# Summed squares as a rounded high and low part, summed behind the fourth weight block; a bank of their own for five first outputs

## The reference

```
def rms_norm(x, w):
    xf = x.astype(jnp.float32)
    y = xf * lax.rsqrt(jnp.mean(xf * xf, axis=-1, keepdims=True) + EPS)
    return (y * w.astype(jnp.float32)).astype(x.dtype)

for layer in range(DEPTH):
    h = rms_norm(x, norm_mix_pre[layer])
    m = mixer_block(h, ...)
    x = x + rms_norm(m, norm_mix_post[layer])
    h = rms_norm(x, norm_ffn_pre[layer])
    f = (silu(h @ w_gate) * (h @ w_up)) @ w_down
    x = x + rms_norm(f, norm_ffn_post[layer])
```

## Time and profile before

| What | us |
|---|---|
| Median of 3 runs (2761.96 to 2762.15) | 2762.11 |
| The profiled execution | 2762.7 |
| Its span, first to last instruction | 2760.9 |
| PE busy | 2743.2 |
| DVE busy | 1517.9 |
| ACT busy | 1051.0 |

### The profile page before, as it was taken

One profiled execution on the slowest core, in us unless ns is written; L12 is line 12 of the kernel. 1 busy time (PEld: TensorE's weight loads), 2 busy tenths in 40 slices (PEclk: granted clock), 3 DMA queues, 4 the chain that ended last, 5 costly groups with the idle time before them and its releaser, 6 DMA issues.

```text
span 2760.9 us, 36069 instructions
## 1 busy us (share of the span) xinstructions
PE 2743.2 (99%) x13580; PEld 2285.3 (83%) x13580; DVE 1517.9 (55%) x2147; ACT 1051.0 (38%) x1462; POOL 57.0 (2%) x59
## 2 busy tenths in 40 slices
PE   9999999999999999999999999999999999999998
PEld 7887888888888888788888888988888877888887
DVE  6944655654434784555565443554434798654433
ACT  5335443432223533633343232332222467432221
POOL 0030000000000003000000000000000000000000
PEclk9999999999999999999999999999999999999999
DMA  4242333233332224133323333233333330233332
GB/s 146 84 125 62 95 92 107 77 108 97 97 98 88 84 88 119 55 102 95 111 76 107 96 91 103 74 113 93 97 97 92 115 106 5 73 114 94 94 99 79
DMA packets 80152, 258.68 MB, mean 94 GB/s; under 512 B 9936, under 2 KB 12368, under 8 KB 79536
## 3 DMA queue, kind: packets, MB, share of 16 engines
q1 hardware_dynamic: 74160, 248.57, 30.2%
q10 hardware_dynamic: 5888, 8.68, 1.2%
HBM read 247.51 MB, written 2.10 MB: 90 GB/s over the span
## 4 chain that ended last, share of the span: by engine, by line
PE 98%; DVE 1%; ACT 1%; issue 0%; DMA 0%; ACTq 0%; DVEq 0%; SPq 0%
PE bank L440 30%; PE bank L441 30%; PE bank L442 30%; PE bank L1344 1%; PE bank L1322 1%; PE bank L1105 1%; PE bank L1308 1%; PE bank L1121 1%; PE bank L1152 1%; DVE w_lo L610 0%; PE bank L1133 0%; PE bank L506 0%; PE bank L514 0%; DVE x L768 0%; ACT w_hi L606 0%
## 5 line engine op out<-in xcount | busy, mean ns | idle before, releaser
L440 PE MATMUL bank<-u_hi,w_hi 128*128 128x512 f32 (+1 forms) x2640 | 1004.3, 380 | 5.4 <-DVE scratch L874 2.7
L441 PE MATMUL bank<-u_lo,w_hi 128*128 128x512 f32 (+1 forms) x2640 | 993.7, 376 | 0.0
L442 PE MATMUL bank<-u_hi,w_lo 128*128 128x512 f32 (+1 forms) x2640 | 993.5, 376 | 0.0
L610 DVE TENSOR_TENSOR w_lo<-raw,w_hi 128x1024 fp32r<-128x1024 f32 x490 | 604.0, 1233 | 616.2 <-ACT w_hi L606 604.8
L606 ACT ACTIVATE w_hi<-raw 128x1024 fp32r<-128x1024 f32 x490 | 514.7, 1050 | 345.8 <-PE bank L442 315.4
L440 PEld LDWEIGHTS bank<-u_hi,w_hi 128*128 128x128 f32 x2640 | 496.9, 188 | 104.8 <-DVE w_lo L610 5.8
L441 PEld LDWEIGHTS bank<-u_lo,w_hi 128*128 128x128 f32 x2640 | 496.9, 188 | 91.3 <-issue 2.4
L442 PEld LDWEIGHTS bank<-u_hi,w_lo 128*128 128x128 f32 x2640 | 496.8, 188 | 91.3
L440 PE MATMUL bank<-hid_hi,w_hi 128*128 128x512 f32 (+1 forms) x792 | 290.1, 366 | 0.0
L442 PE MATMUL bank<-hid_hi,w_lo 128*128 128x512 f32 (+1 forms) x792 | 289.4, 365 | 0.0
L441 PE MATMUL bank<-hid_lo,w_hi 128*128 128x512 f32 (+1 forms) x792 | 289.4, 365 | 0.0
(11 more groups left out here) (273 smaller groups left out, 2594.4 us busy)
## 6 DMA issues: line engine op xcount, KB each, us to landing
raw<-in_weights SPq DMA_DIRECT2D x410, 512.0 KB, 3.5
raw<-in_weights SPq DMA_DIRECT2D x48, 256.0 KB, 2.7
raw<-in_weights SPq DMA_DIRECT2D x32, 384.0 KB, 3.1
rot_s<-rot_in ACTq DMA_DIRECT2D x32, 128.0 KB, 2.3
q_s<-q_in ACTq DMA_DIRECT2D x52, 64.0 KB, 3.0
x<-in_x SPq DMA_DIRECT2D x4, 512.0 KB, 6.6
ret_mask<-in_ret_mask SPq DMA_DIRECT2D x2, 1024.0 KB, 6.0
out<-x SPq DMA_DIRECT2D x16, 128.0 KB, 1.8
```

Source lines behind the costliest of these rows:

```text
L440: nc.tensor.matmul(out, st_hi, mv_hi, start=first, stop=False)
L441: nc.tensor.matmul(out, st_hi, mv_lo, start=False, stop=False)
L442: return nc.tensor.matmul(out, st_lo, mv_hi, start=False, stop=last)
L610: nc.vector.tensor_tensor(w_lo[:, bl.slot(p), :], raw[:, bl.raw(p), :], w_hi[:, bl.slot(p), :].bitcast(F32), ALU.subtract).then_inc(lo_spl ...
```

## The change

Four things are changed.

1. The "pre" sum is no longer a float32 matmul of `acc`. ACT rounds `acc` into `sq_hi[:, 0, :]` (`act_acc_high`), DVE subtracts the rounded part and writes the rest into `sq_hi[:, 1, :]` (`dve_acc_low`), and PE makes two float32r matmuls with `ones_r`. Both new instructions stand behind the split of block 4, and PE waits for the low part before the first of the two.
2. The sum stands behind the whole of block 3, not before its k = 6.
3. The same split is made at each join for the share of `acc` in the half sums; the squares that came last stay in float32.
4. In stages 1, 3, 4, 5 and 6 the stage's first output goes into bank 4 instead of its place in the round; the first matmul itself raises the counter of the bank that is passed over.

`ones_r` is written at the start of layer 0 instead of in each layer's first head copy.

```
+FIRST_BANK = 4
+FIRST_NO = {1: 0, 3: 1, 4: 2, 5: 3, 6: 4}
...
         def pe_sums_pre(pe, key, s, li=None):
             use = side(key, li)
             pe.wait_ge(use.drained, use.n + 1)
-            pe.wait_ge(acc_done.sem, acc_done.upto(s, 7))
-            nc.tensor.matmul(use.mem[:, :], ones_c, acc[:, :], start=True, stop=True).then_inc(use.filled, 1)
+            pe.wait_ge(acc_lo.sem, acc_lo.upto(s, 1))
+            nc.tensor.matmul(use.mem[:, :], ones_r[:, :], sq_hi[:, 0, :], start=True, stop=False)
+            nc.tensor.matmul(use.mem[:, :], ones_r[:, :], sq_hi[:, 1, :], start=False, stop=True).then_inc(use.filled, 1)
...
         def pe_sums_half(pe, key, s, hf, paired, li=None):
-            pe.wait_ge(acc_done.sem, acc_done.upto(s, 13))
-            nc.tensor.matmul(use.mem[:, 0:TH], ones_c, acc[:, cols], start=True, stop=False)
+            pe.wait_ge(acc_lo.sem, acc_lo.upto(s, 2))
+            nc.tensor.matmul(use.mem[:, 0:TH], ones_r[:, :], sq_hi[:, 0, cols], start=True, stop=False)
+            nc.tensor.matmul(use.mem[:, 0:TH], ones_r[:, :], sq_hi[:, 1, cols], start=False, stop=False)
...
+        def first_result(s):
+            return Use(ps[FIRST_BANK], first_out.sem, None, first_out.upto(FIRST_NO[s], -1))
...
         def pe_first(pe, bl, ou, s, sums_b):
+            beside = s in FIRST_NO
...
+                to = ps[FIRST_BANK] if beside and i == 0 else ps[ou.bank(i)]
...
+                    if beside and i == 0 and hf == 0 and k == K_ORDER[0]:
+                        mm.then_inc(drained[ou.bank(0)], 1)
...
+        def act_acc_high(act, s, n):
+            act.wait_ge(acc_done.sem, acc_done.upto(s, 7 if n == 0 else 13))
+            nc.scalar.activation(sq_hi[:, 0, :], acc[:, :], ACT.Copy).then_inc(acc_hi.sem, 1)
+
+        def dve_acc_low(dve, s, n):
+            dve.wait_ge(acc_hi.sem, acc_hi.upto(s, n + 1))
+            nc.vector.tensor_tensor(sq_hi[:, 1, :], acc[:, :], sq_hi[:, 0, :].bitcast(F32), ALU.subtract).then_inc(acc_lo.sem, 1)
...
         def pe_ffn(pe, s, f, bl, ou, pre, post, li=None, more=True):
-            pe_block(pe, bl, 3, ou, 3, u_hi, u_lo, each_k=sums_k)
+            pe_block(pe, bl, 3, ou, 3, u_hi, u_lo)
+            pe_sums_pre(pe, pre, s, li)
...
         def act_ffn(act, s, f, bl, ou, pre, post, li=None, half=False, next_gains=None):
...
                         act_split(act, b, 1 + AHEAD)
+                        act_acc_high(act, s, 0)
                         act_rsqrt(act, pre, li)
-                    act.wait_ge(drained[o.bank(2 * i)], o.uses(2 * i) + 2)
+                    src = first_result(s) if isinstance(j, int) and i == 0 else result(o, 2 * i)
+                    act.wait_ge(src.drained, src.n + 2)
...
         def dve_ffn(dve, s, f, bl, ou, post_gains, next_gains=None):
...
                         dve_split(dve, b, 1 + AHEAD)
+                        dve_acc_low(dve, s, 0)
                         dve.wait_ge(r_done.sem, r_done.upto(s, 1))
-                    use = result(o, 2 * i)
+                    use = first_result(s) if isinstance(j, int) and i == 0 else result(o, 2 * i)
```

More of the change, by code:

```diff
@@ L346, in build @@
         acc_done = ev("acc_done", 13)
+        acc_hi = ev("acc_hi", 2)
+        acc_lo = ev("acc_lo", 2)
         r_done = ev("r_done", 3)
@@ L351, in build @@
         late_out = ev("late_out", 1)
+        first_out = ev("first_out", 1)
         values_out = ev("values_out", 2 * (TT - 1))
@@ L521, in pe_sums_half @@
             mm.then_inc(use.filled, 1)
+        def first_result(s):
+            return Use(ps[FIRST_BANK], first_out.sem, None, first_out.upto(FIRST_NO[s], -1))
         def pe_first(pe, bl, ou, s, sums_b):
+            beside = s in FIRST_NO
+            if s in (1, 3):
+                src = side(f"s{HEADS - 1}0", s // 2)
+                pe.wait_ge(src.drained, src.n + 2)
+            if s == 6:
+                src = side("pt62")
+                pe.wait_ge(src.drained, src.n + 2)
             def add(i, hf, ks):
@@ L532, in add @@
                     w = slice(k * P, (k + 1) * P)
-                    mm = three(ps[ou.bank(i)][:, cols], w_hi[:, b, w], w_lo[:, b, w], u_hi[:, k, cols], u_lo[:, k, cols],
+                    mm = three(to[:, cols], w_hi[:, b, w], w_lo[:, b, w], u_hi[:, k, cols], u_lo[:, k, cols],
                                k == K_ORDER[0], k == K_ORDER[-1])
+                    if beside and i == 0 and hf == 0 and k == K_ORDER[0]:
+                        mm.then_inc(drained[ou.bank(0)], 1)
                     if hf == 1 and k == K_ORDER[-1]:
@@ L779, in dve_join_ffn @@
             dve_last_square(dve, s, KD - 1)
+            dve_acc_low(dve, s, 1)
             use = result(ou, KD - 2)
@@ L819, in pe_ffn @@
             b1, o1 = bl.on(N_UP * UP_TURNS), ou.on(N_UP * UP_TURNS)
+            src = first_result(s)
+            pe.wait_ge(src.drained, src.n + 2)
             for m in range(KD - 1):
@@ L1167, in project @@
                     pe_block(pe, bl, i, ou, i, u_hi, u_lo)
[L1169 to L1173, removed]
+                pe_block(pe, bl, 3, ou, 3, u_hi, u_lo)
+                pe.wait_ge(consts_in, CONSTS)
+                pe_sums_pre(pe, "pre0", s, li)
                 pe.wait_ge(ga_split.sem, ga_split.upto(li, 2))
@@ L1272, in q_var @@
                 nc.tensor.matmul(use.mem[:, :], sq_consts[:, C_BD64, :], sq_h[i % 2][:, :], start=True, stop=True).then_inc(use.filled, 1)
-            def sums_k(k):
-                if k == 6:
+            for i in range(3, 14):
+                pe_block(pe, bl, i, ou, i, u_hi, u_lo)
+                if i == 3:
                     pe_sums_pre(pe, "pre3", 5)
-            for i in range(3, 14):
-                pe_block(pe, bl, i, ou, i, u_hi, u_lo, each_k=sums_k if i == 3 else None)
                 if 4 <= i <= 8:
@@ L1282, in _ @@
                 if i == 4:
+                    src = first_result(5)
+                    pe.wait_ge(src.drained, src.n + 2)
                     pe_turn_r(pe, "tm3", 5)
@@ L1383, in head_copy @@
                 act.wait_ge(hn_sq.sem, hn_sq.upto(li, n + 1))
-                if n == 0:
-                    nc.scalar.activation(ones_r[:, :], ones_c, ACT.Copy)
                 nc.scalar.activation(sq_hi[:, n % 2, :], sq_h[n % 2][:, :], ACT.Copy).then_inc(hn_hi.sem, 1)
@@ L1461, in layer @@
                 split(1)
+                if li == 0:
+                    act.wait_ge(consts_in, CONSTS)
+                    nc.scalar.activation(ones_r[:, :], ones_c, ACT.Copy)
+                act_acc_high(act, s, 0)
                 act_rsqrt(act, "pre0", li)
@@ L1586, in q_square @@
             def q_square(i):
-                act.wait_ge(drained[ou.bank(i)], ou.uses(i) + 2)
+                src = first_result(5) if i == 0 else result(ou, i)
+                act.wait_ge(src.drained, src.n + 2)
                 nc.scalar.activation(sq_h[i % 2][:, :], q_in[:, i % Q_IN, :], ACT.Square).then_inc(q_sq.sem, 1)
@@ L2053, in _ @@
                 if i < 14:
-                    use = result(ou, i)
+                    use = first_result(5) if i == 0 else result(ou, i)
                     dve.wait_ge(block_done, bl.n(i) + (RING + 1))
```

8 lines of the change are left out of this document (5 added, 3 removed).

## The result

| | us |
|---|---|
| Before, median of 7 runs on the same chip | 2762.12 (2761.96 to 2762.52) |
| After, median of 7 runs | 2771.31 (2768.43 to 2773.16) |
| Ratio, 95% interval | 1.0031 (1.0022 to 1.0041) |
| Profiled execution of after, and its span | 2768.43, 2766.7 |

The change makes the kernel slower by 9.2 us, 0.3%. The forecast was 2766.0 with a range up to 2769.5: wrong by 5.3 us, and outside its range. The runs also spread: seven runs of before lie within 0.6 us, those of after within 4.7. That spread is the first hint that something was added which happens in some runs and not in others. The mean granted clock of each run goes with it: 0.998 in the three fastest runs of after, 0.997 in the next three, 0.996 in the slowest, where all runs of before on record have 0.999.

A forecast was written before the change was run, and what follows sets the result against it. PE, busy 99% of the span, was taken as the bound. Nets +5.0, layer 1 +1.8, layer 0 +0.2, attention -1.1 and half sums -2.0 gave +3.9 us, so 2766.0; range 2761.5 to 2769.5.

The forecast's parts named there:

- The chain in the nets, +1.25 each: Stages 1, 3, 4, 6: chain of r starts 1.25 us later, so block 5's split holds PE; four times, +5.0.
- Layer 1, +1.8: Stage 2: PE waits for the low part behind block 4's late split; the sum costs 2.75 us against 0.92.
- Layer 0, +0.2: Stage 0: the sum waits for the low part and costs 1.06 us against 0.86.
- Attention, -1.1: Stage 5: block 4's second matmul at 2159.37 instead of 2160.47; bounds -1.4 and 0.
- The half sums, -2.0: Joins: 0.20 us saved in each of seven halves a and three halves b; bounds 0 and -2.8.
- The base: Whole kernel: profiled execution 2762.7 plus 3.9 gives 2766.6; the median, 0.6 lower, gives 2766.0.
- at 0.91 for a sum and 0.48 for a half: Float32 sums on PE by the skill's four passes; rows gave 0.86 and 0.43; end result would be 0.4 us lower.
- "The clock falls", 3%, 2793: Rival: PE stands 2.2 to 2.4 us five times and the clock drops to 1.2 GHz behind it; 2793, 3%.
- stayed up for about half of that window: Kernel's end, last 11 us, mean granted clock 0.76: read as the clock falling only when PE rests for long.
- The price, 5.5 us for one block: Behind each of five stalls, one block at the lower clock level would take 5.5 us more.

The follow-up runs named there:

- Experiment 4: Kernel before with only the bank of its own for the stages' first outputs: 2761.34 us, ratio 0.9997.
- experiment 5: Kernel before with only the half sums of the joins changed to high and low parts: 2760.49 us, ratio 0.9994.
- experiment 2: Kernel after with ten unused matmuls before block 4 in each of four nets and nine before layer 1's sum: 2766.89 us, ratio 1.0017.
- experiment 1: Kernel after with ten unused matmuls between the sum and block 4 in each of the four nets: median 2768.5 us, ratio 1.0021.
- experiment 6: Kernel before with only the pre sum's place changed to behind block 3, still one float32 matmul: 2771.27 us, ratio 1.0034.
- experiment 7: Kernel after without the bank of its own, first outputs back in the round: 2772.4 us, ratio 1.0043.
- experiment 3: Kernel after with block 5 of each net split early, right behind the high and low part of acc: 2756.96 us, ratio 0.9983.
- experiment 9: Kernel after with the pre sum back before k = 6 of block 3, still of high and low part: 2772.58 us, ratio 1.0038.

## Why the prediction was wrong

Point by point, by its own steps:

- **The chain in the nets, +1.25 each: right.** Forecast for block 5 in stage 1 was 556.11, less 0.4 from the two half sums ahead; measured 555.73. The wait moved from block 4 to block 5, on the split, 2.2 us each, as said. Experiment 4 shows the same refill without the new sum.
- **Layer 1, +1.8: right**, with a rest of 2.31 for the 2.2 forecast. **Layer 0, +0.2**: at the next join half a's sum had not moved (-0.02). **Attention, -1.1: right** within 0.2; its sum waits 0.41.
- **The half sums, -2.0: right** within 0.3. Alone they give 1.7 (experiment 5). In after one of them gave nothing, half a behind stage 3, which is half of what stage 4 has over its forecast.
- **The base.** The forecast is the median of before, 2762.1, and +3.9. With the rests filled (experiment 2) the change costs 4.7 by medians and 2765.1 - 2760.9 = 4.2 by the spans of the profiled executions. The 0.5 between comes from before's profiled execution, which lies 0.6 above its median where that of experiment 2 lies at its own; what made it longer stays open. So 0.9 of the error of 5.3 us lies in the chain and the base, and 4.4 in the clock.
- **A small slip**: at 0.91 for a sum and 0.48 for a half, the prediction says, the result would be 0.4 us lower. With 0.05 for each of the ten halves and of the three sums outside the nets it would be 0.65. Nothing hangs on it.
- **"The clock falls", 3%, 2793: this is the step that failed**, in chance and in price. Its premise was right, five rests of 2.2 to 2.4 us, and stood in the text; the clock then got no term in the sum, and a rest was priced at its own length alone. Experiments 1 and 2 take 4.4 us away with nothing but work in those rests. By the single fall of the profile, 1.6 us, and the level without falls, 2766.9, the seven runs of after (1.5 to 6.3 us above it) had about one to four each: roughly every second rest.
- **Where the argument was faulty.** It rested on the earlier trace rows: a mean granted clock of 0.76 over 11 us at the kernel's end, of which the prediction took that the clock "stayed up for about half of that window", and so would outlast rests of 2.4 us. That window holds one long rest, at its end, and says how late the clock fell there once: full for some 5.7 of the 11 us, so about 3.5 us behind the last matmul. The same end of the kernel, in the profile of experiment 2, shows another delay; its last matmul ends at 2756.34:

```profile
2756.40:2757.90 1.50, 0.00 (x0) 0.00 (x0) 0.66 (x2) 0.78 (x2) 0.00 (x0) 1.00 0.00 0
2758.00:2765.00 7.00, 0.00 (x0) 0.00 (x0) 4.75 (x15) 0.00 (x0) 0.00 (x0) 0.50 0.44 150
```

There the clock fell 1.6 us behind the last matmul, in after 2.1, and in all twelve profiles of this document from 1.5 to 4.7. One reading of a delay that spreads so far is no lower bound. Before's waits had no rest of over 1.3 us inside the work to judge by. A case that no row shows wanted a chance like a coin's, not 3%. The Trainium skill, "TensorE: Matmul & The Clock Gate", section "HAM oscillation — how this bites in real kernels", gives as its rule a length that idle gaps of PE should not exceed, and that length is greater than any of the five rests. Taken as a bound it would have called rests of 2.2 us harmless, and the traces disagree: the clock fell behind rests of 2.1 to 2.3 us (0.50 in after, 0.51 in experiment 1, 0.50 in 6 and 7).
- **The price, 5.5 us for one block, was too large** by a factor of more than three. The lower level lasts some 3.4 us, and half of it is lost: the trace of after gives 1.6, the groups of runs in experiments 1 and 3 give 1.8 and 1.6.

Put together with the measured sizes: 4.7 for the chain and, at two or three falls of 1.6, some 4.4 for the clock make the 9.2. With the clock's term at half a chance (5 x 0.5 x 1.6 = 4.0) the forecast would have been 2770.

## What to carry to other kernels

Ask of every wait that a change makes longer not only how long the engine stands, but what TensorE's clock does behind it: in this kernel each rest of over 2 us brought, beside its own length and about every second time (an estimate from the runs' times), 1.6 us more. A bank or a buffer that lifts a wait gives nothing while the next wait of the same chain is just covered: look where the chain is met again, and shorten or reorder the chain (here, by splitting block 5 first, 10 us) before adding room. Ask too whether the chain starts late for more than one reason, here the place of the sum and the place of the low part: putting the sum back alone gave the nets nothing. When the runs of a changed kernel spread while those of before don't, look for the granted clock window by window, since the mean hides it (0.998 to 0.999).

## What the runs showed of the hardware

- **The granted clock fell behind rests of 2.1 to 2.3 us, in some runs and places and not in others**: all five of the profiled after were of about that length, and one was followed by a fall. The same rest of 2.3 us in layer 1 brought a fall in nine of eleven runs of experiment 1 and in five of eleven of experiment 3, by their times. Behind 3.7 us the runs agree with a fall each time. Behind rests within the work of 1.85 us and less no profile shows one (six of 1.45 to 1.85 us in experiment 9, one of 1.3 us in every profile).
- **A fall costs about the same each time**: 1.6 us in the trace of after, 1.8 and 1.6 between the two groups of runs in experiments 1 and 3. The moment at which it begins isn't tied to PE's return: about 0.1 us ahead of the first matmul in experiment 7 (the window at the lower level begins at 550.00, the matmul starts at 550.14), two or three matmuls behind it in after, 1.4 us behind it in experiment 6 (2166.6 for 2165.23).
- **Matmuls that do nothing useful can make a kernel faster**: 49 of them, in five places, gave 4.4 us (experiment 2).
- **A float32 matmul can be replaced by two float32r ones in about half the time**: the acc share of a half sum takes 0.24 us, where it took 0.43. From the start of a half sum its reader on ACT comes 0.19 earlier (516.87 to 518.36 before, 516.84 to 518.14 after).
